# Strassen's seven block products for the input projection of the banded block, over two halves of 1024 tokens

## What is computed

```python
a = _rmsnorm(h, g_in[i])
z = jnp.einsum('bsd,de->bse', a, w_in[i])        # 2048 x 1024 times 1024 x 3584
q, k, v, gate_b, u_a, v_a, gate_a = jnp.split(z, ..., axis=-1)   # seven parts of 512 columns
q = _rope(_rmsnorm(q.reshape(B, S, N_HEADS, HEAD_DIM), q_norm[i]), positions)   # k the same
# silu(gate_b), silu(gate_a), gelu(u_a), layernorm(gelu(v_a)) are applied further on
```

## Time and profile before

| | us |
|---|---|
| three runs, median (lowest to highest) | 4332.2 (4326.4 to 4332.87) |
| profiled execution, time | 4326.4 |
| its span, first to last instruction | 4326.4 |
| TensorE matmul busy | 3967.8 (92%) |
| VectorE busy | 2036.2 (47%) |
| ScalarE busy | 1432.6 (33%) |
| GpSimd busy | 683.4 (16%) |
| mean granted TensorE clock | 0.957 |

### The profile page before, as it was taken

One profiled execution on the slowest core, in us unless ns is written; L12 is line 12 of the kernel. 1 busy time (PEld: TensorE's weight loads), 2 busy tenths in 40 slices (PEclk: granted clock), 3 DMA queues, 4 the chain that ended last, 5 costly groups with the idle time before them and its releaser, 6 DMA issues. The chain is left out here.

```text
span 4326.4 us, 66533 instructions
## 1 busy us (share of the span) xinstructions
PE 3967.8 (92%) x25359; PEld 3241.8 (75%) x25359; DVE 2036.2 (47%) x4616; ACT 1432.6 (33%) x3255; POOL 683.4 (16%) x761
## 2 busy tenths in 40 slices
PE   6999999899679799999999869799999989979799
PEld 4777789777568688778977658677777867868687
DVE  5365111167656542111127567632750456657554
ACT  5000444256422310144327523321111467721211
POOL 3021000223120210000032220131430001000100
PEclk8999999999889899999999989899999989989899
DMA  5244221731256422222273345432111143357221
GB/s 195 90 147 143 82 77 61 230 136 59 100 196 220 175 100 73 95 76 77 75 240 106 113 146 198 173 112 90 64 71 66 47 134 102 103 214 255 79 77 64
DMA packets 215264, 525.90 MB, mean 122 GB/s; under 512 B 27478, under 2 KB 88392, under 8 KB 205604
## 3 DMA queue, kind: packets, MB, share of 16 engines
q1 hardware_dynamic: 188740, 438.91, 29.2%
q0 software_dynamic: 26208, 82.74, 5.4%
HBM read 330.43 MB, written 191.13 MB: 121 GB/s over the span
## 5 line engine op out<-in xcount | busy, mean ns | idle before, releaser
L72 PE MATMUL tm_tacc<-tm_tw_hi,hT_hi 128*128 128x384 f32 (+1 forms) x1120 | 414.6, 370 | 17.2 <-DVE tm_tw_lo L906 10.0
L73 PE MATMUL tm_tacc<-tm_tw_lo,hT_hi 128*128 128x384 f32 (+1 forms) x1120 | 410.0, 366 | 0.0
L74 PE MATMUL tm_tacc<-tm_tw_hi,hT_lo 128*128 128x384 f32 (+1 forms) x1120 | 410.0, 366 | 0.0
L72 PE MATMUL tz_tacc<-tz_tw_hi,hT_hi 128*128 128x512 f32 x896 | 359.4, 401 | 6.0 <-POOL tz_tw_lo L935 4.1
L72 PE MATMUL cm_acc<-hT_hi,cm_wb_hi 128*128 128x512 f32 (+1 forms) x912 | 362.2, 397 | 0.0
L73 PE MATMUL tz_tacc<-tz_tw_lo,hT_hi 128*128 128x512 f32 x896 | 355.0, 396 | 0.0
L74 PE MATMUL tz_tacc<-tz_tw_hi,hT_lo 128*128 128x512 f32 x896 | 355.0, 396 | 0.0
L74 PE MATMUL cm_acc<-hT_hi,cm_wb_lo 128*128 128x512 f32 (+1 forms) x912 | 344.3, 378 | 0.0
L73 PE MATMUL cm_acc<-hT_lo,cm_wb_hi 128*128 128x512 f32 (+1 forms) x912 | 343.9, 377 | 0.0
L788 DVE SCALAR_TENSOR_TENSOR tm_ds<-tm_dg,tm_ds 128x512 f32<-128x512 f32 (+1 forms) x40 | 25.6, 639 | 532.1 <-ACT tm_ds L782 532.1
L72 PEld LDWEIGHTS tm_tacc<-tm_tw_hi,hT_hi 128*128 128x128 f32 x1120 | 210.9, 188 | 59.1 <-DVE tm_tw_lo L906 13.6
(11 more groups left out here) (405 smaller groups left out, 8770.1 us busy)
## 6 DMA issues: line engine op xcount, KB each, us to landing
scr_z<-tz_tz SPq DMA_DIRECT2D x112, 256.0 KB
scr_zcm<-cm_zo SPq DMA_DIRECT2D x96, 256.0 KB, 2.0
scr_ztm<-tm_tz SPq DMA_DIRECT2D x68, 256.0 KB, 2.0
scr_xres<-out_x POOLq DMA_DIRECT2D x34, 512.0 KB, 4.1
cm_area<-in_w_ada POOLq DMA_DIRECT2D x64, 256.0 KB, 3.0
scr_z<-out_xn POOLq DMA_DIRECT2D x32, 512.0 KB, 4.8
mo_z<-scr_z SPq DMA_DIRECT2D x16, 1024.0 KB
tz_traw<-in_w_in SPq DMA_DIRECT2D x7, 2048.0 KB, 8.4
```

Of the source, the lines that this page charges most:

```text
L72: nc.tensor.matmul(out, ah, bh, start=start, stop=False)
L73: nc.tensor.matmul(out, ah, bl, start=False, stop=False)
L74: return nc.tensor.matmul(out, al, bh, start=False, stop=stop)
```

## The change

`project_z` takes the place of `project_tm` in this phase. The 2048 tokens are two halves of 1024. In each half, A is the tokens (2 x 2 blocks of 512 tokens by 512 channels) and B a chunk of 512 weight columns (2 x 2 blocks of 512 channels by 256 columns). The four output blocks of 512 tokens by 256 columns come from seven block products, not eight, in the Strassen-Winograd form with left factors A11, A12, S2, S3, S1, S4, A22 (S are sums and differences of A's blocks, made once in a half) and right factors made of B's blocks for each chunk.

- A pass over a half and 512 columns is a chunk `cc`; there are 14. A product `i` (0 to 6) has two units `d` of 256 tokens. A unit is 2 token tiles x 4 slices x 3 matmuls of 256 columns.
- Each left factor is split once in a half (`rounded` on ScalarE, `rest` on VectorE; `take` scales the transposed tokens). Each right factor is split once in a chunk: hi by `high` (ScalarE, 128x1024), lo by `low` (VectorE, 128x1024). GpSimd makes four differences of B's blocks in a chunk (`differences`, 128x1024 each) and S1 and S2 (`sums`); VectorE makes S3 and S4 (`third`, `fourth`).
- PSUM holds products 0+1, 2+3, 4+5 and 6 in three pairs of banks. Units of products 0 and 1 are read by ScalarE, those of 2 to 6 by VectorE (`read`, 128x512, PSUM plus SBUF).
- The q and k chunks have four groups of 128x1024 each: `head_sums`, `heads` (VectorE), `rotate` (GpSimd), `square` and `root` (ScalarE). The v_a chunk has `stats` and `normed` (VectorE). They are placed by product in each engine's loop.
- Weights are loaded in quarters of 512 KB, in each half anew; tokens in 1024 KB (`tokens`); output in 512 KB.

In the diff, lines of "..." stand for what is left out.

```diff
--- before.py
+++ after.py
+class TwoByTwo:
+    A11, A12, S2, S3, S1, S4, A22 = range(7)
+    OPENS = (True, False, True, False, True, False, True)
+    BANK = (0, 0, 1, 1, 2, 2, 3)
+def product(nc, out, lhsT, rhs, first, last):
+    (ah, al), (bh, bl) = lhsT, rhs
+    nc.tensor.matmul(out, ah, bh, start=first, stop=False, skip_group_check=True)
+    nc.tensor.matmul(out, ah, bl, start=False, stop=False, skip_group_check=True)
+    return nc.tensor.matmul(out, al, bh, start=False, stop=last, skip_group_check=True)
+def project_z(nc, io, keep, stored):
...
+    parts = [[3, 2, 0, 6, 1, 5, 4], [4, 2, 0, 6, 1, 5, 3]]
+    NCP = 7
+    chunks = [(h, seg) for h in range(2) for seg in parts[h]]
+    NCC, NM = len(chunks), 7 * len(chunks)
+    heads_at = [cc for cc, (h, seg) in enumerate(chunks) if seg < 2]
+    norm_at = [cc for cc, (h, seg) in enumerate(chunks) if seg == 6]
...
+        bank = lambda cc, i, d: 1024 * ((8 * cc + 2 * W.BANK[i] + d) % 3)
+        pair_of = lambda cc, i, d: acc[:, bank(cc, i, d):bank(cc, i, d) + 1024].rearrange("p (a n) -> p a n", n=512)[:, :, 0:256]
+        duo = lambda x, d: x[:, 2 * d:2 * d + 2, :]
+        group = lambda cc, j: 4 * cc + j
+        out_of = lambda cc, j: outs[group(cc, j) % 5]
...
+                def tokens(load):
...
+                    if load > 4:
+                        sp.wait_ge(tp_ok, 4 * load)
...
+                def products(cc, i, d):
+                    h, m = chunks[cc][0], 7 * cc + i
+                    if d == 0:
+                        pe.wait_ge(w_lo, m + 1)
+                    if cc % NCP == 0:
+                        pe.wait_ge(a_ok, split_no(h, i, d))
+                    if i == 0 and cc >= 1:
+                        pe.wait_ge(ev_dve, dve_read(cc - 1, 4, 0) if d else dve_read(cc - 1, 3, 1))
+                    if i == 1:
+                        pe.wait_ge(ev_act, act_read(cc, 0, d))
+                    if i == 2 and d == 0 and cc >= 1:
+                        pe.wait_ge(ev_dve, dve_read(cc - 1, 4, 1))
+                    if i == 2 and d == 1:
+                        pe.wait_ge(ev_act, act_read(cc, 1, 0))
+                    if i == 3:
+                        pe.wait_ge(ev_dve, dve_read(cc, 0, d))
+                    if i == 4:
+                        if d == 0:
+                            pe.wait_ge(ev_act, act_read(cc, 1, 1))
+                        else:
+                            pe.wait_ge(ev_dve, dve_read(cc, 1, 0))
+                    if i == 5:
+                        pe.wait_ge(ev_dve, dve_read(cc, 2, d))
+                    if i == 6:
+                        pe.wait_ge(ev_dve, dve_read(cc, 3, 0) if d else dve_read(cc, 1, 1))
+                    for x in range(2):
+                        p = slice(128 * (2 * d + x), 128 * (2 * d + x + 1))
+                        at = bank(cc, i, d) + 512 * x
+                        for k in range(4):
+                            last = product(nc, acc[:, at:at + 256], (hi[i][:, k, p], lo[i][:, k, p]),
+                                           (wh[m % 3][:, k, :], wl[m % 3][:, k, :]), W.OPENS[i] and k == 0, k == 3)
+                    last.then_inc(mm_ok, 1)
+                turn(0, range(4))
+                turn(1, range(4))
+                for cc in range(NCC):
+                    for i in range(7):
+                        if cc == 0 and i in (1, 2):
+                            turn(i + 1, range(4))
+                        for d in range(2):
+                            if cc == LAST and 2 <= i <= 5:
+                                turn(i + 2, (2 * d, 2 * d + 1))
+                            products(cc, i, d)
...
+                def differences(cc, x):
+                    b11, b21, b12, b22 = [quad[(4 * cc + y) % 6][:, :, :] for y in range(4)]
+                    if x == 0:
+                        for y in (0, 2):
+                            pool.wait_ge(q_in[(4 * cc + y) % 6], 16 * ((4 * cc + y) // 6 + 1))
+                        pool.wait_ge(w_lo, 7 * cc + 1)
+                        nc.gpsimd.tensor_tensor(b11, b12, b11, ALU.subtract).then_inc(t_ok, 1)
+                    if x == 1:
...
+                def rotate(cc, j):
+                    n, b = heads_no(cc, j), j in (1, 3)
+                    x = out_of(cc, j).rearrange("p a (h d) -> p a h d", d=HD)
+                    table = lambda w: turns[:, w, 4 * b:4 * b + 4, None, :].to_broadcast([128, 4, 4, 32])
+                    pool.wait_ge(n_ok, n + 1)
+                    nc.gpsimd.tensor_tensor(part_pool, x[:, :, :, 0:32], table(3), ALU.mult).then_inc(tp1_ok, 1)
+                    pool.wait_ge(td_ok, n + 1)
+                    nc.gpsimd.tensor_tensor(x[:, :, :, 32:64], x[:, :, :, 32:64], table(2), ALU.mult).then_inc(tp1_ok, 1)
+                    pool.wait_ge(tp1_ok, 2 * n + 2)
+                    nc.gpsimd.tensor_tensor(x[:, :, :, 32:64], x[:, :, :, 32:64], part_pool, ALU.add).then_inc(y_pool, 1)
...
+                for cc in range(NCC):
+                    for i in range(7):
+                        if i == 1 and cc - 1 in heads_at:
+                            rotate(cc - 1, 2)
+                        if i == 3 and cc - 1 in heads_at:
+                            rotate(cc - 1, 3)
+                        if i == 4 and cc in heads_at:
+                            rotate(cc, 0)
+                        if i == 5 and cc == LAST:
+                            sums(1, 0)
+                            sums(1, 1)
+                        if i == 5 and cc + 1 < NCC:
+                            differences(cc + 1, 0)
+                            differences(cc + 1, 1)
+                        if i == 6 and cc + 1 < NCC:
+                            differences(cc + 1, 2)
+                            differences(cc + 1, 3)
+                        if i == 6 and cc in heads_at:
+                            rotate(cc, 1)
...
+                def rest(h, op, q):
...
+                def low(m):
+                    if m < NM:
+                        dve.wait_ge(w_hi, m + 1)
+                        vec.tensor_tensor(wl[m % 3][:, :, :], source(m // 7, m % 7)[:, :, :], wh[m % 3][:, :, :].bitcast(F32), ALU.subtract).then_inc(w_lo, 1)
+                def read(cc, i, d):
+                    e, src = i - 2, pair_of(cc, i, d)
+                    dve.wait_ge(mm_ok, unit(cc, i, d) + 1)
+                    if i == 2:
+                        dve.wait_ge(ev_act, act_read(cc, 0, d))
+                        vec.tensor_tensor(duo(u2, d), duo(u3, d), src, ALU.add).then_inc(ev_dve, 1)
+                        return
+                    if i == 3:
+                        vec.tensor_tensor(duo(u3, d), duo(u3, d), src, ALU.add).then_inc(ev_dve, 1)
+                        return
+                    j = i - 3
+                    if group(cc, j) >= 5:
+                        dve.wait_ge(stored_out[group(cc, j) % 5], 16 * (group(cc, j) // 5))
+                    dve.wait_ge(ev_dve, dve_read(cc, 0 if i == 5 else 1, d))
+                    vec.tensor_tensor(duo(out_of(cc, j), d), duo(u2 if i == 5 else u3, d), src, ALU.add).then_inc(ev_dve, 1)
...
+                def heads(cc, j):
+                    n, b = heads_no(cc, j), j in (1, 3)
+                    rows = out_of(cc, j).rearrange("p a (h d) -> p (a h) d", d=HD)
+                    x = out_of(cc, j).rearrange("p a (h d) -> p a h d", d=HD)
+                    table = lambda w: turns[:, w, 4 * b:4 * b + 4, None, :].to_broadcast([128, 4, 4, 32])
+                    dve.wait_ge(sr_ok, n + 1)
+                    vec.reciprocal(ss[:, 1, :], ss[:, 1, :])
+                    dve.drain()
+                    vec.tensor_tensor(rows, rows, ss[:, 1, :, None].to_broadcast([128, 16, HD]), ALU.mult)
+                    dve.drain().then_inc(n_ok, 1)
+                    vec.tensor_tensor(part_dve, x[:, :, :, 32:64], table(1), ALU.mult).then_inc(td_ok, 1)
+                    dve.wait_ge(tp1_ok, 2 * n + 1)
+                    vec.tensor_tensor(x[:, :, :, 0:32], x[:, :, :, 0:32], table(0), ALU.mult)
+                    dve.drain()
+                    vec.tensor_tensor(x[:, :, :, 0:32], x[:, :, :, 0:32], part_dve, ALU.subtract).then_inc(y_dve, 1)
...
+                for b in range(2, 4):
+                    take(b, 0)
+                    take(b, 2)
+                    fourth(0, b - 2)
+                    rest(0, W.S2, b - 2)
+                for cc in range(NCC):
+                    for i in range(7):
+                        for d in range(2):
+                            if d == 0:
+                                low(7 * cc + i + 2)
+                            if cc == 0:
+                                if i == 1:
+                                    third(0, d)
+                                    rest(0, W.S3, d)
+                                elif 2 <= i <= 4:
+                                    rest(0, (W.S1, W.S4, W.A22)[i - 2], d)
+                            if cc == LAST:
+                                if 2 <= i <= 5:
```

(57 more changed lines are left out.)

483 lines of the change are left out of this document (475 added, 8 removed).

## The result

The changed kernel takes **4385.0 us** (median of four runs, 4377.2 to 4389.3) against 4332.5 for the kernel before (four runs): the ratio is 1.0123, 95% interval 1.0108 to 1.0137. It is slower by 52.5 us. Forecast were 4366, also slower, in a range (up to 4412) that holds it. The profiled execution took 4385.7, its span is 4383.9.

The account below looks back on a forecast made before the run. TensorE, busy 94 to 95 of 95 us, was taken to bound the phase; 42 + 562.3 + 76 + 33 + 6 = 719.3 us for 685.6, 33.7 more, gave 4366; range from 4302 less 6 to 4412.

Parts of the forecast that it names:

- Matmuls: Whole phase: 4704 matmuls of 256 columns at 0.1195 us each take 562.3 us, 64.9 less than before.
- Start: Phase start: first product at 19.5 us, then transposes, a chain of left factors and half clock; 42 us, 34 to 50.
- The 9.4 us ahead of product 2: First chunk: TensorE idle 9.4 us while product 2 waits for `low(2)` behind GpSimd sums, `fourth`, `rounded` and `rest`.
- q, k and v_a chunks: VectorE, blocked by GpSimd, paces these products and TensorE waits; 38 us a half, 76 in all.
- 34 if VectorE wins: q, k and v_a chunks: of 42 us of waits a half, some 8 less if VectorE wins the port each time.
- That is 18 over, before the differences and before any wait: 21 products around the q/k chunks: VectorE has 139 us of work against 121.
- Change of halves: Between the halves: token loads, transposes, a chain behind GpSimd's sums and differences, blocking and clock; 33 us, 22 to 45.
- End: Phase end: no layer norm, only a read, an activation and a 512 KB store; 6 us for 10.9.
- Rival A: q, k and v_a chunks: VectorE and GpSimd steps interleave, stalls only 20 us; 4302 us; chance 0.28 including results up to no change.
- rival B: Much worse stalls, long waits bringing half clock and reads falling behind for whole chunks: 110 us for 76; 4417 us; chance 0.10.
- The signs that the prediction named: Profile: spacing 0.12, read waits 60 to 100 us, slower rotation and differences, waits of 8 to 10 and 7, plain chunks under 42.
- part 3's lower bound: q, k and v_a chunks: VectorE and GpSimd never block each other, `heads` is 3.7, and 10 us a half remain.

Follow-up runs that it names:

- e4: Changed kernel with all head and norm work of the q, k and v_a chunks left out; 4307.9 us.
- e7: Changed kernel with VectorE instead of GpSimd summing S1 and S2 of the first half, and `low(2)` taken earlier; 4375.3 us.
- e8: Changed kernel with GpSimd's `rotate` of the second group placed ahead of the next chunk's last two weight differences; 4372.1 us.
- e10: Changed kernel with the edits of e9 and e7 together; 4348.4 us.
- e11: e10 with some reads ahead of `low`, square and sum earlier, last norm step moved, angle tables spread over chunk 0; 4304.7 us, 0.9951 of the kernel before.
- e9: Changed kernel with head and norm steps moved away from tight reads, chunks reordered, angle tables in chunk 0; no operation removed; 4359.4 us.
- e2: Changed kernel without GpSimd's four weight differences per chunk, plain blocks of B in their place; 4358.6 us.
- e6: Changed kernel with VectorE's head step cut in two at its wait for GpSimd, which keeps its part of the rotation; 4378.4 us.

## Why the prediction was right, and where it was not

The direction and the place were right. The size was right in the sum, but in its main term by two misses that cancel, and one of the reasons counted for much less than the prediction gave it.

1. **Matmuls**: 40.3 us in a plain chunk, also 160 us of them in a row (e4). So 562.3 stands. The estimate on a line between the two figures of the Trainium skill's "TensorE: Matmul & The Clock Gate", Back-to-back issue gap, 98 ns at 256 columns, disagrees with the 120 measured, as its 131 did with the 233 at 512. By the measured pair the change saves 64.9 us. By the Trainium skill's, an estimate, it would have cost 109.

2. **Start**: 52.0 for 42, the largest miss of the sum. The 9.4 us ahead of product 2 came by the forecast's links, but were 11.7: GpSimd's sums took 2.34 to 2.40, then `fourth` 3.25 beside a difference of GpSimd where I had put 1.2. Product 3's wait was 3.7 for 2.8. A further 1.2 us is a wait for a rest. The other two terms were too small. Inside the units the matmuls of chunk 0 lost 5.0 us to the half clock, for 2: by windows,

```profile
2834.00:2887.60 53.60, 35.16 (x248) 34.24 (x249) 34.38 (x34) 20.70 (x24) 15.63 (x7) 0.78 0.18 54
```

the granted clock is 0.78 in most of it. And the transposes of loads 2 and 3 with their waits took 10.5 (2.4 and 8.1) for 8. e7 shows that 7.5 us of the start were the order.

3. **q, k and v_a chunks**: 77.9 for 76, the nearest of the terms that were open, and in part by luck. The 38 of a half were waits alone (42 laid out by hand, 34 if VectorE wins), with the half clock at nothing in the sum. TensorE's waits are 25.1 us in chunks 2 to 5 and 27.1 in 9 to 12, a third less. Its matmuls inside the units lose 11.6 and 10.0 us at the lower clock, and the last 2 of each half's 39 lie between units. So "as VectorE and not TensorE paces these products" did not hold for the clock: behind most waits of over 2 us its matmuls run slowly for about a unit, and this adds to the wait. The places were right. Waits were forecast ahead of product 5 in chunk 2 and ahead of products 3 and 5 in chunks 3, 4 and 5, and all of these are there. Their sizes were mostly too large: 3.5 came at 2.1; 9 and 5.5 at 4.4 and 1.8; 5.4 and 5.2 at 3.2 and 6.8; 9 and 4 at 2.9 and 0.8. Up to 2.3 us ahead of product 1 were not forecast.

   Of the reasons, "`heads` stands between the two reads of product 4, 6, 1 or 3, and product 3 waits for the reads of product 2, 5 for those of 4" is borne out: e4 shows that the stalls come with these steps, and e8 and above all the way from e10 to e11 (49.8 us lost, then 10.0) that moving them is enough. "That is 18 over, before the differences and before any wait" was 9 over (129.8 us busy for 120.5), in part because I had priced all 16 head steps at 7.2 us where twelve take 5.8 or 6.1 and four 10.3 (mean 6.9). It does not account for 38 us a half. But it isn't void either: in that order of chunks the work of the 21 products does not fit, held time counted. e11 doesn't refute it, since it has the same steps over 31 products, and its fullest 21 hold 105.4 us. How much of the way from 82 to 44 us in e9 is the spreading and how much the places stays open.

4. **Change of halves**: 37.7 for 33, within its bounds. By TensorE's starts and waits in chunks 6 and 7 it is 9.5 us of waits for three token loads (10.5 forecast), 8.7 of transposes (5), 10.7 ahead of the first units of the new half (12.7; in place of 7.5 before the second unit there are 3.3 before the first and 3.4 before the second), and 8.9 of half clock (5). e2, without the differences, has 1.8 and nothing for the 3.3 and 3.4, which bears out the chain through them. e11 keeps 36.

5. **Chunk 1**: 4.3 us behind the angle tables, which I had put nowhere. In e11, where they are spread over chunk 0, chunk 1 loses 2.6 with head steps of its own. **End**: 6.1 for 6.

The misses, 10.0 + 4.3 + 1.9 + 4.7 and 0.8 of small ones, are the 21.7 between 741.0 and 719.3. Rival A named the right condition (stalls under 21 us a half) but the wrong means: the engines went on taking turns in e11, and the stalls are 5 a half all the same. Of rival B, the half clock behind long waits came, the spreading of waits over whole chunks did not.

The signs that the prediction named came out mixed. The spacing of 0.12 is there. So are the stretched rotation products (means of 2.0, 1.0 and 1.6 us for L2907, L2909 and L2911) and differences (up to 3.4). TensorE's waits for VectorE's reads are 53.7 us in total, under the 60 to 100. The wait before product 2 is 11.7, not 8 to 10, and the one of 7 before the second half's second unit is 3.4. Chunk 1, named as a plain one, takes 44.5 us, over the 42 at which the prediction would have been wrong. Its matmuls are not dearer, though: chunk 8 takes 40.3. The lower bound of the range is given there in two ways that disagree: A less 6 is 4296, part 3's lower bound with the rest at the middle is 4310. The result lies far above both.

## What to carry to other kernels

When an engine that isn't full holds up the one that is, first add up its work over the stretch. If it does not fit (here 129.8 us in 120.5), the stretch can't pass without a loss, and the work has to be spread. A sum that fits promises nothing yet: e10 still lost 49.8 us. Then write down for each of its instructions what it releases and by when: in these runs a step delayed TensorE only where it stood ahead of something due sooner. A change that cuts the matmuls of an accumulation may bring reads that are due one unit after their data. Such reads want to be first on their engine. Look at the list of waits again after each move: the next read in line shows up only then.

## What was not expected of the hardware

- In these traces long VectorE operations that read SBUF twice stood until the instruction of GpSimd beside them had ended, and then took about their full time: a 128x1024 one takes 1.21 us alone and 3.26 beside one difference (L2820). Even four small scalings of 128x256 (L2937 in e9), 0.41 each alone, took 6.78 us together beside three differences (one of them 2.5). Reads of PSUM were not held: 0.67 to 0.69 us in all 140 of every run, as in the earlier trace rows.
- The granted clock falls for waits that are themselves cheap. After 4.41 us of idle time the next unit of 24 matmuls took 5.0 us from its first to its last start in place of 2.8, the 1.2 GHz level. In e11, with waits of 1.3 us at most, the granted clock of chunks 1 to 5 is 1.00, for 0.93 in chunks 2 to 5 of the changed kernel. Not every wait does it: in e7 the unit behind a wait of 2.11 us took 2.9 us in chunk 2 and 4.3 in chunk 9.
- A load of a function table on ScalarE takes 1.28 us, and I had counted all of them as hidden. In e6 one stood in the chain that product 2's second unit waited for.
